# Prompt columns of the first two up tiles around the last sample's values, sample columns and latent sample products behind them

## The reference, cut to what matters

```python
def decoder_layer(x, c, pos, attend, lw):
    mod = jax.nn.silu(c) @ lw['w_ada'] + lw['b_ada']
    shift_m, scale_m, gate_m, shift_f, scale_f, gate_f = jnp.split(mod[:, None, :], 6, axis=-1)
    h = rms_norm(x, lw['g_norm_mix']) * (1 + scale_m) + shift_m
    mla_t, dsa_t = mixer_projections(h, pos, lw)
    o_mla, o_dsa = attend(mla_t, dsa_t)
    x = x + gate_m * merge_groups(o_mla, o_dsa, lw['g_out'], lw['w_out'])
    h = rms_norm(x, lw['g_norm_ffn']) * (1 + scale_f) + shift_f
    x = x + gate_f * swiglu(h, lw['w_ffn_in'], lw['w_ffn_out'])
    return x, rows

def swiglu(h, w_ffn_in, w_ffn_out):
    g, u = jnp.split(h @ w_ffn_in, 2, axis=-1)
    return (jax.nn.silu(g) * u) @ w_ffn_out
```

## Time and profile before

| | us |
|---|---|
| median of three timed runs | 1254.75 |
| lowest and highest of them | 1250.54, 1258.36 |
| the profiled execution, its own time | 1252.33 |
| span in its profile | 1250.5 |
| mean granted TensorE clock over the span | 0.957 |

### The profile page before, as it was taken

One profiled execution on the slowest core, in us unless ns is written; L12 is line 12 of the kernel. 1 busy time (PEld: TensorE's weight loads), 2 busy tenths in 40 slices (PEclk: granted clock), 3 DMA queues, 4 the chain that ended last, 5 costly groups with the idle time before them and its releaser, 6 DMA issues.

```text
span 1250.5 us, 22534 instructions
## 1 busy us (share of the span) xinstructions
PE 1184.0 (95%) x9176; PEld 1060.3 (85%) x9176; DVE 675.5 (54%) x1508; ACT 396.9 (32%) x772; POOL 92.5 (7%) x138
## 2 busy tenths in 40 slices
PE   6699999998999999999999999989999999979997
PEld 4588896465687899999999888879999999959997
DVE  0643853745888787778867342342433343294330
ACT  3322333532577655555555123311001011000001
POOL 2000002001105300000000121000000000000000
PEclk9799999987999999999999999659999999999999
DMA  9597651022001202222232565302332323133321
GB/s 323 133 281 201 192 170 52 1 68 73 29 17 61 77 1 77 77 77 77 77 127 85 193 207 208 135 1 85 96 89 85 99 84 100 57 93 93 93 69 68
DMA packets 137739, 129.10 MB, mean 103 GB/s; under 512 B 17110, under 2 KB 131171, under 8 KB 135580
## 3 DMA queue, kind: packets, MB, share of 16 engines
q1 hardware_dynamic: 133596, 86.89, 23.5%
q0 software_dynamic: 4064, 41.11, 9.0%
HBM read 124.58 MB, written 3.41 MB: 102 GB/s over the span
## 4 chain that ended last, share of the span: by engine, by line
PE 82%; DVE 9%; DMA 3%; ACT 3%; issue 2%; SPq 0%; POOL 0%; DVEq 0%; ACTq 0%
PE psV L1166 19%; PE psV L950 13%; PE psA L1166 10%; PE psA L687 7%; PE psV L1062 4%; PE psV L887 2%; PE psA L1045 2%; PE psA L1113 2%; PE psA L930 2%; PE psV L911 2%; PE psV L643 2%; PE psV L749 2%; PE psA L1000 1%; PE psA L898 1%; PE psA L1036 1%
## 5 line engine op out<-in xcount | busy, mean ns | idle before, releaser
L950 PE MATMUL psV<-r_r,wide_r 128*128 128x260 f32 x1536 | 207.5, 288 | 3.3 <-DVE msk L1987 2.7
L950 PEld LDWEIGHTS psV<-r_r,wide_r 128*128 128x128 f32 x1536 | 190.4, 189 | 5.9 <-issue 3.3
L1445 ACT ACTIVATE wring<-psV 128x512 f32<-128x512 f32 x128 | 76.1, 596 | 91.5 <-PE psV L950 69.1
L1166 PE MATMUL psV<-qiz_r,wring_r 128*128 128x260 f32 x528 | 93.9, 283 | 0.0
L2183 DVE TENSOR_TENSOR wide<-wide,psV 128x520 f32 (+1 forms) x22 | 15.3, 696 | 138.4 <-PE psV L1166 138.4
L1988 DVE TENSOR_REDUCE msk<-wring 128x8 f32<-128x512 f32 x128 | 86.4, 675 | 0.0
L687 PE MATMUL psA<-wide_r,wring_r 128*128 128x260 f32 x432 | 79.8, 289 | 6.5 <-DVE hT_r L2225 6.4
L1166 PEld LDWEIGHTS psV<-qiz_r,wring_r 128*128 128x128 f32 x528 | 76.2, 188 | 0.0
L1166 PE MATMUL psA<-qiz_r,r_r 128*128 128x260 f32 x352 | 71.7, 285 | 1.6 <-DVE hT_r L2120 1.6
L1166 PE MATMUL psA<-hT_r,r_r 128*128 128x260 f32 x352 | 71.5, 285 | 0.0
L1166 PE MATMUL psA<-qiz_r,wring_r 128*128 128x260 f32 x352 | 71.4, 285 | 0.0
(11 more groups left out here) (490 smaller groups left out, 2600.2 us busy)
## 6 DMA issues: line engine op xcount, KB each, us to landing
wring<-w_ffn_in SPq DMA_DIRECT2D x44, 512.0 KB, 3.8
wide<-w_ada SPq DMA_DIRECT2D x11, 1024.0 KB, 6.8
wring<-w_ffn_out SPq DMA_DIRECT2D x16, 704.0 KB, 4.7
tok<-w_ada SPq DMA_DIRECT2D x9, 1024.0 KB, 7.6
wring<-w_in SPq DMA_DIRECT2D x24, 256.0 KB, 3.4
wring<-w_out SPq DMA_DIRECT2D x8, 512.0 KB, 8.4
wide<-w_out SPq DMA_DIRECT2D x2, 2048.0 KB, 8.3
wring<-w_in SPq DMA_DIRECT2D x20, 128.0 KB, 2.7
```

Source lines behind the costliest of these rows:

```text
L950: mm = pe.matmul(kx[m % 2][:, hf, :], w, wtab[:, b % 2, l, 2 * k + hf, :], start=(k == 0 and w is high and l == 0), stop=(k == 1 and w is ...
L1166: mm = pe.matmul(out[:, hf, 0:HT], w[:, k, :], x[:, hf * HT:(hf + 1) * HT], start=(k0 + k == 0 and x is xh and w is high), stop=(k0 + k == ...
L1445: A(sq2[m % 2].rearrange("p (x n) -> p x n", x=2), kx[m % 2][:, :, 0:256], ACT.Square).then_inc(kx_squared, 1)
```

## The change

Five things change.

- TensorE's list: up tile x of the first turn is now multiplied in two parts. The new `up_prompt(x, k0, k1)` does the 512 prompt columns of the k from k0 to k1, in halves of 260 and 252 columns; the samples' 8 columns are done in `pe_tail` once they exist, 24 matmuls a tile. The pieces stand where the code says: tile 0, k 0 to 3, before the last `weigh_values`; k 4 and 5 behind it; k 6 and 7 behind the last `values_out`; tile 1 behind the sample products, around the samples' sum. Gate tiles 0 and 1 follow the samples' columns.
- Both groups of sample products stand behind all of tile 0.
- VectorE and ScalarE modulate the prompt earlier: tiles 0 and 1 stand ahead of the last sample's scores, tile 7 behind `od_full`.
- VectorE splits all four weight tiles of the first turn in the sample loop (up 0, up 1, then gate 0, gate 1), and the first `gate_turn` leaves its own two out.
- `spm`, where the sample products go, lies in another PSUM bank, and the padding of the slots' parity is done by counting a semaphore up by one more in place of the 1x1 matmuls.

TensorE's list around the last sample, before: the names are those of the tiles, xN says how many follow in a row.

The diff, cut:

```diff
@@ build
-        spm = psA[:, 1, 1, 160:288].rearrange("p (m g b) -> p m g b", m=8, g=2)
+        spm = psA[:, 1, 0, 0:128].rearrange("p (m g b) -> p m g b", m=8, g=2)
@@ pe_decode
+            def up_prompt(x, k0, k1):
+
+                s = 2 * x + 1
+                if k0 == 0:
+                    pe.wait_ge(w_split, 9 + x)
+                    pe.wait_ge(v_free, V_U + x - 1)
+                for k in range(k0, k1):
+                    pe.wait_ge(x_split, KD + k + 1)
+                    high, low = pieces(whigh[s])[:, k, :], pieces(wlow[s])[:, k, :]
+                    for w, xx in ((high, xhigh), (high, xlow), (low, xhigh)):
+                        for hf, c, n in ((0, 0, HT), (1, HT, SEQ - HT)):
+                            pe.matmul(sv(V_U + x)[:, hf, 0:n], w, xx[:, k, c:c + n], start=(k == 0 and w is high and xx is xhigh),
+                                      stop=(k == KD - 1 and w is low), skip_group_check=True)
...
                 if b == NB - 1:
-                    pe.wait_ge(ol_taken, 2)
-                    pe.wait_ge(wo_loaded[0], 16)
-                    for m in range(KD):
-                        sample_out(0, m)
+                    up_prompt(0, 0, 4)
                 weigh_values(b)
...
+            up_prompt(0, 4, 6)
             values_out(NB - 1)
+            up_prompt(0, 6, 8)
+            pe.wait_ge(ol_taken, 2)
+            pe.wait_ge(wo_loaded[0], 16)
+            for m in range(KD):
+                sample_out(0, m)
             pe.wait_ge(wo_loaded[1], 16)
...
             mm.then_inc(od_full, 1)
+            up_prompt(1, 0, 4)
             pe.wait_ge(s_summed, 1)
-            pe.matmul(ssum_ffn, ones, sum8, start=True, stop=True, skip_group_check=True).then_inc(a_full, 1)
+            pe.matmul(ssum_ffn, ones, sum8, start=True, stop=True, skip_group_check=True).then_inc(a_full, 1 + PADA)
+            up_prompt(1, 4, 8)
@@ pe_tail
             pe.wait_ge(x_split, 2 * KD + 1)
-            ffn_turn(0)
+            for x in range(2):
+                for k in range(KD):
+                    high, low = pieces(whigh[2 * x + 1])[:, k, :], pieces(wlow[2 * x + 1])[:, k, :]
+                    for w, xx in ((high, xhigh), (high, xlow), (low, xhigh)):
+                        mm = pe.matmul(sv(V_U + x)[:, 1, SEQ - HT:HT], w, xx[:, k, SEQ:T], start=(k == 0 and w is high and xx is xhigh),
+                                       stop=(k == KD - 1 and w is low), skip_group_check=True)
+                mm.then_inc(v_full, 1)
+            for x in range(2):
+                pe.wait_ge(w_split, 11 + x)
+                pe.wait_ge(a_free, A_G + x - 1)
+                passes(pieces(wlow[2 * x]), pieces(whigh[2 * x]), proj, sa(A_G + x)).then_inc(a_full, 1)
@@ act_decode
             for b in range(NB - 1):
+                if b == 6:
+                    high_part(0)
+                    high_part(1)
                 take(NB + b)
...
-                    high_part(0)
+                    high_part(2)
...
+            high_part(3)
             A(stat[0:1, 0, 2:3], epsc[0:1], ACT.Sqrt)
-            high_part(1)
-            high_part(2)
+            high_part(4)
+            high_part(5)
             take(2 * NB - 1)
-            for k in range(3, 7):
-                high_part(k)
+            high_part(6)
+            high_part(7)
@@ dve_decode
                 elif b <= 5:
-                    split_tile(v, 2, b - 4)
+                    split_first(v, 2 * (b - 4) + 1, 8 + b - 4)
...
+                if b == 5:
+                    split_first(v, 0, 10)
+                    split_first(v, 2, 11)
                 if b == 6:
...
+                    modulate_prompt(v, 0)
+                    modulate_prompt(v, 1)
-            modulate_prompt(v, 3)
-            modulate_prompt(v, 4)
+            modulate_prompt(v, 5)
+            modulate_prompt(v, 6)
             v.wait_ge(od_full, 1)
...
-            modulate_prompt(v, 5)
-            modulate_prompt(v, 6)
+            modulate_prompt(v, 7)
+            modulate_prompt(v, 8)
             v.wait_ge(a_free, A_MIX + 1)
...
-            modulate_prompt(v, 7)
             link(v.tensor_tensor(hs, xs, amod[:, 1, :, 1:9], ALU.mult))
-            modulate_prompt(v, 8)
...
+        def split_first(v, s, n):
+
+            split(v, wraw[s], wlow[s], whigh[s], tail_w[s], 48, n)
@@ dve_tail
-            def gate_turn(i, ahead):
+            def gate_turn(i, ahead, first=0):
 
                 for s in range(2):
-                    if s == 0 or ahead:
+                    if s >= first and (s == 0 or ahead):
...
-            with v.Fori(0, KF // 2 - 1) as i:
+            gate_turn(0, True, 1)
+            with v.Fori(1, KF // 2 - 1) as i:
                 gate_turn(i, True)
```

More of the change, by code:

```diff
@@ L1074, in prompt_sums @@
                 if c4 == 3:
-                    mm.then_inc(v_full, 1)
+                    mm.then_inc(v_full, 1 + PADV)
             def k_scores(b, tile=None, sums=False):
@@ L1171, in pe_tail @@
             proj = lambda k: (xhigh[:, k, :], xlow[:, k, :])
[L1173 to L1178, removed]
             def ffn_turn(i, need=None):
@@ L1513, in prompt_root @@
             def prompt_root():
-                act.wait_ge(v_full, V_SS2 + 1)
+                act.wait_ge(v_full, V_SS2 + 1 + PADV)
                 act.wait_ge(v_free, V_SS2)
-                A(root2, psV[:, 1, 0, :], ACT.Sqrt, scale=1.0 / D, bias=epsc[:]).then_inc(v_free, 1)
+                A(root2, psV[:, 1, 0, :], ACT.Sqrt, scale=1.0 / D, bias=epsc[:]).then_inc(v_free, 1 + PADV)
             def high_part(k):
@@ L1553, in act_decode @@
                     prompt_square(2 * b - 1)
+            high_part(3)
             A(stat[0:1, 0, 2:3], epsc[0:1], ACT.Sqrt)
-            high_part(1)
-            high_part(2)
+            high_part(4)
+            high_part(5)
             take(2 * NB - 1)
-            for k in range(3, 7):
-                high_part(k)
+            high_part(6)
+            high_part(7)
             act.wait_ge(a_full, A_MIX + 1)
             A(rms8.rearrange("p g b -> p (g b)"), ssum_mix, ACT.Sqrt, scale=1.0 / 512, bias=epsc[:]).then_inc(a_free, 1)
-            high_part(7)
-            act.wait_ge(a_full, A_SS2 + 1)
-            A(root8, ssum_ffn, ACT.Sqrt, scale=1.0 / D, bias=epsc[:]).then_inc(a_free, 1)
+            act.wait_ge(a_full, A_SS2 + 1 + PADA)
+            A(root8, ssum_ffn, ACT.Sqrt, scale=1.0 / D, bias=epsc[:]).then_inc(a_free, 1 + PADA)
         def act_tail(act):
             A = nc.scalar.activation
-            if PADA:
-                act.wait_ge(a_full, A_SS2 + 2)
-                A(stat[0:1, 0, 0:1], sa(A_SS2 + 1)[0:1, 0, 0:1], ACT.Identity).then_inc(a_free, 1)
             with act.Fori(0, KF // 2) as i:
@@ L2063, in dve_decode @@
                 elif b == NB - 1:
-                    modulate_prompt(v, 0)
+                    modulate_prompt(v, 2)
                 shift(NB + b)
                 if b == NB - 1:
-                    modulate_prompt(v, 1)
+                    modulate_prompt(v, 3)
                 row_sums(NB + b)
@@ L2073, in dve_decode @@
                 elif b <= 5:
-                    split_tile(v, 2, b - 4)
+                    split_first(v, 2 * (b - 4) + 1, 8 + b - 4)
                 elif b == NB - 1:
-                    modulate_prompt(v, 2)
+                    modulate_prompt(v, 4)
                 normalise(NB + b)
@@ L2086, in dve_decode @@
                     latent_values()
+                if b == 5:
+                    split_first(v, 0, 10)
+                    split_first(v, 2, 11)
                 if b == 6:
-                    v.wait_ge(v_free, V_SS2 + 1)
+                    v.wait_ge(v_free, V_SS2 + 1 + PADV)
                     link(v.reciprocal(root2, root2))
-            modulate_prompt(v, 3)
-            modulate_prompt(v, 4)
+                    modulate_prompt(v, 0)
+                    modulate_prompt(v, 1)
+            modulate_prompt(v, 5)
+            modulate_prompt(v, 6)
             v.wait_ge(od_full, 1)
@@ L2110, in dve_decode @@
             v.tensor_reduce(sum8, sq64.rearrange("p k b -> p b k"), AXX, ALU.add).then_inc(s_summed, 1)
-            modulate_prompt(v, 7)
             link(v.tensor_tensor(hs, xs, amod[:, 1, :, 1:9], ALU.mult))
-            modulate_prompt(v, 8)
-            v.wait_ge(a_free, A_SS2 + 1)
+            v.wait_ge(a_free, A_SS2 + 1 + PADA)
             link(v.reciprocal(root8, root8))
@@ L2167, in add_gated @@
                 v.tensor_tensor(x[:, SEQ:T], x[:, SEQ:T], gated[:, s, :], ALU.add).then_inc(x_new, 1)
-            if PADV:
-                v.wait_ge(v_full, V_SS2 + 2)
-                v.tensor_copy(stat[0:1, 0, 1:2], sv(V_SS2 + 1)[0:1, 0, 0:1]).then_inc(v_free, 1)
-            def gate_turn(i, ahead):
+            def gate_turn(i, ahead, first=0):
                 for s in range(2):
-                    if s == 0 or ahead:
+                    if s >= first and (s == 0 or ahead):
                         for c in range(2):
```

## The result

The changed kernel takes **1261.01 us** (median of 20 runs, 1256.78 to 1265.23), the kernel before 1254.22 (20 runs on the same chips, 1250.54 to 1258.36). The ratio is 1.0053, 95% interval 1.0041 to 1.0064: 6.8 us slower. That is within the 1% of the forecast's "same", but the sign is wrong and the time lies 0.5 us above the range. The profiled execution took 1260.68 us (span 1258.9), 8.4 more than that of before.

A forecast was written before the change was run, and what follows sets the result against it. TensorE was taken to bound the kernel: what it executes, waits for, or executes at half clock. Terms from 801.1 us summed to 61.4 us against 62.6, 1.2 less, giving 1253.6 us; range 1246.5 to 1260.5.

The forecast's parts named there:

- (6): Sample products, 128 records plus 2 of sums: full clock for 4 us, then half; 23.9 us, ends 28.1 and 19.2.
- (5): Behind the last values_out: an added wait for VectorE's modulation, then the last 12 matmuls of up tile 0; 3.8 us.
- (1) to (4): 24 early up tile 0 matmuls, last values, 12 matmuls over ScalarE's copy, values_out: 4.3, 1.2, 1.4, 0.4 us.
- (7): First 24 matmuls of up tile 1, behind the sample products: half clock for 3.2 us again; 4.3 us.
- (8): Samples' sum, 0.2 us, and 24 more up tile 1 matmuls, 2.9 us, covering the VectorE tail before the gates.
- (9): 48 added 8-column matmuls at 0.11 us: 5.3 us, bounds 2.6 and 10.4; 7.0 with a clock fall inside counted.
- (10): Two gate tiles after the sample columns, at 5.77 us each: 11.5 us.
- (11): Weights: gate tile 0's ring slot is refilled late; 0.5 us of waiting, 2.0 on top if two loads share engines evenly.
- A: Rival: once raised near 804 us, the clock stays up through all 8-column work; 1240.3 us; 5%.
- B: Rival: the 8-column fp32r matmul costs half and the clock does not fall inside the 48; 1249.2 us; 12%.
- C: Rival: up tile 0's pieces do not hold or lift the clock; 1262.3 us, far end 1270.8; 8%, half at far end.
- D: Rival: the late slot refill becomes a real wait and one clock level falls badly; 1256.6 us; 20%.

The follow-up runs named there:

- columns twice: Changed kernel with its 48 added 8-column sample matmuls issued a second time; 1271.55 us, ratio 1.0149 to the kernel before.
- two of the 48 left: Changed kernel with one sample-column matmul per up tile, 2 instead of 48, so results are incomplete; 1251.64 us, ratio 0.9984 to the kernel before.
- columns between gates: Changed kernel with the 48 sample-column matmuls placed three at a time between the six gate matmuls of each k; 1257.28 us, ratio 1.0032.
- modulation ahead: Changed kernel with VectorE's modulation steps 7 and 8 moved ahead of its wait for od_full; 1255.07 us, ratio 1.0009 to the kernel before.
- latent first: Changed kernel with the latent sample products ahead of the last 12 matmuls of up tile 0; 1259.67 us, ratio 1.0046 to the kernel before.
- halves: Against the changed kernel: columns 0 to 259 of all four first-turn tiles multiplied early, 260 to 519 later, no matmuls added; 1246.63 us, ratio 0.9925.
- repaired: Changed kernel with both VectorE modulation ahead of the od_full wait and sample-column matmuls between gate matmuls; 1251.45 us, ratio 0.9979 to the kernel before.
- dense matmuls dealt out: As halves, but 36 early 260-column matmuls dealt out between the latent sample products; 1248.07 us, ratio 0.9947 to the kernel before.

## Why the prediction was wrong

**The step that failed is (6).** It took full clock for 4 us over the sample products, 23.9 us in all, with 28.1 as the upper end. Measured: 20.29 + 0.44 + 6.81 = 27.5 us, all at half. The bound came from the 8.4 us after the last 512-column matmul; its lower end, nothing, was named, and the range did reach 4 us up from there, but the forecast sat in the middle. The first products ran at half from their first record. In all five profiles that have the change's order up to the products (the changed kernel and its repetition, columns twice, two of the 48 left, columns between gates) the clock fell 1.8 to 2.5 us before the products began: at 813.6 for 815.6, 808.4 for 810.3, 811.1 for 813.6, 812.1 for 813.9 and 812.0 for 813.9 us. Without the wait it fell after they began: by 2.4 us (modulation ahead), 2.1 (latent first), 4.4 (halves), 4.7 (repaired). So 4 us of full clock was nearly right for an order that has no wait, and I had put the wait in front of it myself, in (5). The wait did this at the least by using up full clock: in all five profiles the spell lasted 6.8 us, 2.2 of them idle. Whether it also shortens the spell is not shown, since without it two profiles had 6.8 us and two 10.3. The row that my bound came from held a warning. In those 8.4 us TensorE also waited, and 2.1 us after it the clock fell:

```profile
789.05 1.06 PE L1045 MATMUL psA<-qd,r 128*128 128x8 f32 x8 [1.83 <-ACT r L1471]
```

TensorE was busy for 3.87 of the 6.20 us in front of that fall, and for 4.52 of 6.70 in front of the fall at 813.6. The prediction counted this row as full clock kept in spite of a wait.

**(5)** foresaw the wait, 2.2 us measured as forecast, but priced it as idle time alone. The 12 matmuls behind it were to take 1.4 at full clock and took 2.54: 4.7 in place of 3.8. Together (5) and (6) are 4.5 of the 7.4 us between my sum, 61.4, and the 68.8 measured. The experiment prices the wait at 5.9 us by medians, not 2.3.

**(1) to (4)** held: 4.78, 1.21, 1.62 and 0.35 us for 4.3, 1.2, 1.4 and 0.4, and no wait for the modulation. The clock rose 3.8 us after 802.9 for my 3.2. **(7)** 5.06 for 4.3: here the rise took 4.6 us from 843.1. **(8)** 3.0 for 3.1; the tail in front of the first gate tile did vanish under tile 1.

**(9)** 48 matmuls at 0.11 and a fall of the clock inside them: the price per matmul was right (0.107), the fall came, and was undersized. The load records that it was argued from (188 and 192 ns) show likeness to the f32 product only; each lasts longer than such a matmul takes, so the record is not itself the price. I had 7.0 with the time behind; (9) and (10) together measured 6.92 + 7.37 + 5.77 = 20.1 us for 18.5. The fall came 3.3 us into them, so some 17 of the 48 took twice their price (3.5 us at 0.213), and the gate tile started cold. **(11)** 0.4 us of waiting for 0.5, on the chain through the slot's load and split as forecast.

**The rivals.** A is refuted: 29.30 of 29.30 us busy at 0.50, with some 130 of the 140 matmul records 8 or 16 columns wide; the page "TensorE: Matmul & The Clock Gate" of the Trainium skill ("Why this matters for your kernels") ties the full clock to a TensorE kept busy, and this stretch does not agree, since it stayed at half with TensorE busy throughout. B is refuted by the 0.107 us; the same page's 25 ns between narrow matmuls ("Back-to-back issue gap") is not met by any row of an 8-column matmul, and the section itself says that its gap leaves the weight loads out, which the prediction passed over. C named the right side and nearly the time (1262.3), and half its mechanism: its test, clock still 0.50 at 808, came out against it, since tile 0 lifted the clock at 806.8. What it also said, that these pieces, "cut by 34 narrow records and the wait", do not hold the clock, is what happened. I gave it 8% because I weighed the lifting, for which there was a row, and never the holding across the wait. D did not come. And the range stopped at 1260.5 although (6)'s own upper end, alone, gave 1253.6 + 4.2, and (9)'s to 10.4 another 3.4: 1261.2, both ends named and both unknown, outside the range.

**Not settled.** Why latent first gained only 1.3 us. Why the same order keeps the clock for 6.8 us in one execution and 10.3 in another. Whether the wait shortens a spell of full clock or only idles in it. An order that keeps it full over all 128 product records was not found; dealing more dense matmuls over both groups was not tried.

## What to carry to other kernels

Price a wait in front of a long run of narrow matmuls with the full clock that goes by in it: here 2.2 us of idling cost 5.9. To fill a hole with work whose last columns are not there yet, cut at a boundary that the matmuls already have (halves: 7.2 us below the kernel before by medians, 0.75% by the ratio) rather than shave 8 columns off, since each shaving is one more matmul, here 0.107 us for 8 columns where one of 260 takes 0.120; where it must be, deal them out among dense ones. And before a block is moved, look at what it stood over: the latent products had hidden 3.6 us of softmax.

## What the runs showed of the hardware

Three things that I had not expected. The clock falls with TensorE busy all the time when the work is 8 columns wide (3.3 us into the 48 fp32r matmuls, each 0.107 us with its weight load at full clock and 0.213 at half), but three such matmuls for every six of 260 columns left it at 1.00 over 16.8 us, at the same price, 5.3 us for the 48. A fall can come behind a wait even when dense work has resumed: 813.6, with 260-column matmuls running since 813.04. And where it had risen, full clock lasted 6.8 us in both profiles of the changed kernel, and as long again from 847.7 to 854.5, 6.8 or 10.3 without the wait, 10.3 in halves and 13.6 with dense matmuls dealt out.
